# Two stage boundaries of a fused transformer kernel: processed by halves of the tokens instead of all tokens at once

## The chip, the cores and the metric

The kernel runs on one core of a Trainium2 chip. Its time is the device time in microseconds (us) of one execution; the median of 3 runs was 1045.91 us. The engines of a core work side by side, each through its own list of instructions in order, and wait for one another through counters (semaphores): TensorE (PE in the profile; PEld is its loading of stationary operands), VectorE (DVE), ScalarE (ACT), GpSimd (POOL), and SyncE (SP), which issues most of the DMA transfers here.

## The reference, cut to what matters

A sequence of 256 tokens of width 1024 goes through two blocks, each of two layers. All is float32.

```python
def first_block(x, ...):
    for l in range(2):
        x = hybrid_layer(x, ...)           # ends in: x = x + square(relu(h2 @ w_up)) @ w_down
    return rmsnorm(x, g_final)

def second_block(x, pre_norm_g, post_norm_g, ...):
    for i in range(2):
        h = rms_norm(x, pre_norm_g[i])
        y = even_mixer(h, ...) if i == 0 else odd_mixer(h, ...)
        x = x + rms_norm(y, post_norm_g[i])
    return x

def even_mixer(h, w_in, ...):
    z = h @ w_in                           # 1024 x 3072: six groups of 512 columns
    ...                                    # attention, pooling, gates
    return concatenate([att, pool]) @ w_out

def odd_mixer(h, w_in, ...):
    z = h @ w_in                           # 1024 x 2560: su, gc, ca, cb, gd of 512 columns each
    ...                                    # su goes into a state space scan, ca/cb into a convolution
    return concatenate([ssm_out, conv_out]) @ w_out
```

The "first boundary" is what lies between the last product of the first block (w_down of layer 1) and the even mixer's first product: the residual sum, rmsnorm with g_final, rms_norm with pre_norm_g[0]. The "second boundary" lies between the even mixer's w_out and the odd mixer's first product (su): rms_norm with post_norm_g[0], the residual sum, rms_norm with pre_norm_g[1].

## The kernel before, in words

The 256 tokens are two tiles of 128 tokens (`T = 2`); x and h lie in the core's memory with tokens on the partitions. Every product is made of pieces: a piece is a 512 x 512 block of a weight matrix, loaded by one DMA of 1 MB into one of four raw places. Since a fast float32r product alone is not exact enough, ScalarE copies a piece to a rounded upper part `w_hi` (line 1154), VectorE makes the remainder `w_lo = raw - w_hi` (line 1494; for the few pieces in `POOL_PIECES` GpSimd does it, line 2156), and TensorE adds three products: hi*hi, hi*lo and lo*hi. There are three places for split pieces (`SPLIT_RING = 3`), so ScalarE may split piece p only when TensorE has used up piece p - 3. In the ScalarE and VectorE programs `step(p)` splits piece p + 2. That order is written out by hand and strictly kept: an engine that waits at one instruction holds up all that stand behind it.

The activations need the same: `turn_rows` transposes h on TensorE (line 813; 16 transposes of 128 x 128 into four banks, each bank holding both token tiles), `turn_hi` on ScalarE (line 1182) copies the banks to `hT_hi` and `turn_lo` on VectorE (line 1515) writes the remainder `hT_lo`, both multiplying by the norm's factor g, which after the transposition is one number for each partition (`gain=V_PRE`).

Products come in two forms. In `tokens_out` the stationary operand is a 128 x 128 block of hT (one token tile) and 512 columns of the weights move past it, 128x512 a time. In `features_out` the stationary operand is a 128 x 128 block of the weights and the 256 tokens move past it, 128x256 a time; its result has features on the partitions. For a piece `tokens_out` makes 12 matmuls for each token tile (4 blocks by 3 products), and `features_out` 48 (4 by 4 by 3).

At the first boundary (pieces of the last `mlp_down`, then E_PIECE and E_PIECE + 1): for each half c of the columns VectorE adds tile 0, then tile 1 to x (line 1750) and multiplies by g_final (1756); ScalarE sums the squares of both (1172, 1349); `final_means` turns these into two means (lines 1665 to 1669), GpSimd takes the roots (line 2007), `final_rows` scales h (1675). TensorE meanwhile makes 12 products of a constant (`keep_clock`, line 780), and then waits for h. Behind the boundary ScalarE splits E_PIECE + 2, takes an exponential for the state space part (line 1357), and VectorE writes x = xg * rstd (line 1767).

At the second boundary (pieces E_OUT_PIECE to E_OUT_PIECE + 3, then O_PIECE and O_PIECE + 1): the result of w_out comes in two halves c of the columns, two pieces each. `post_squares` on ScalarE (line 1408) and `post_norm` on VectorE (1870, 1879) handle half 0 of both tiles, split three pieces, and handle half 1 of tile 0 and of tile 1. Then `squares` (1172), the root (2007), and the scaling of h (1890). TensorE transposes the matrices of the state space part (1039, 1044), runs 11 `keep_clock` products, and transposes h. The first product is su, by `features_out`, with `drive(0)` (1063) in it: 16 small products that start the state space part. VectorE answers each `drive(j)` with `turn_back(j)` (1908 to 1914) and `scan(j)` (1923); before `turn_back(0)` stand the splits of O_PIECE + 2 and O_PIECE + 3.

Of the kernel before, what the change touches and what calls it, by code (L numbers as in the profile page):

```python
# [94 lines left out]
POOL_PIECES = (O_PIECE + 4, O_PIECE + 5, O_PIECE + 8, O_OUT_PIECE, O_OUT_PIECE + 1)  # L95
# [8 lines left out]
V_MIX, V_MLP, V_PRE, V_LRE, V_LIM, V_PSC, V_D, V_GLUB, V_LNG, V_LNB, V_ROWS = (  # L104
    0, 16, 32, 48, 64, 80, 84, 88, 96, 100, 104)
# [50 lines left out]
def build_program(nc, ins, consts, where, out):  # L156
    ctx = ExitStack()
    with ctx:
# [55 lines left out]
        final_inv = sb("final_inv", [P, T])  # L214
        ret_ss = sb("ret_ss", [P, T, RET_HEADS])
# [99 lines left out]
        g_post = [area(10240, D), area(0, D)]  # L315
        conv_out = area(8192, HALF, SEQ)
# [21 lines left out]
        ROWS_T = [bank[:, i, :] for i in (6, 7, 3, 4)]  # L338
        ACC = [[bank[:, 2, :], bank[:, 3, :]], [bank[:, 4, :], bank[:, 5, :]]]
# [9 lines left out]
        poolw_landed = sem("poolw_landed")  # L349
        gpost_landed = [sem(f"gpost_landed{i}") for i in range(DEPTH)]  # L350
# [164 lines left out]
        def stat_count(n, t):  # L515

            return T * (n if n <= 2 * DEPTH else n - 1) + t + 1

# [68 lines left out]
        def _(sp):  # L587
# [4 lines left out]
            def small_inputs():  # L592
# [5 lines left out]
                vector_rows(V_PRE, ins["pre_norm_g_2"].rearrange("l d -> (l d)"))  # L598
# [27 lines left out]
            for l in range(DEPTH):  # L626
# [9 lines left out]
                for f in range(-2, F_GROUPS):  # L636
                    if l == DEPTH - 1 and f == 0:
                        for t in range(T):
                            sp.wait_ge(out_free[t], l * USES + USE_UP)
                        sp.dma_start(g_final, ins["g_final"].partition_broadcast(P)).then_inc(gfinal_landed, 16)  # L640
                        for b, w in enumerate(("o_b_re_2", "o_b_im_2")):
                            sp.dma_start(b_in[:, b, :, :], ins[w][0].rearrange("(s g) p i -> (g p) s i", g=2)).then_inc(s5_landed, 16)
# [19 lines left out]
            sp.dma_start(g_post[0], ins["post_norm_g_2"][0].partition_broadcast(P)).then_inc(gpost_landed[0], 16)  # L662
            for g in range(5):
# [28 lines left out]
        def _(pe):  # L692
# [131 lines left out]
            def turn_vectors():  # L824

                pe.wait_ge(rows_landed, 16 * 9)
# [111 lines left out]

            def mlp_down(l, f):
# [15 lines left out]
            for l in range(DEPTH):  # L955
# [25 lines left out]
                for f in range(F_GROUPS):  # L981
                    mlp_down(l, f)
# [4 lines left out]
            keep_clock(6, 12)  # L987
            turn_rows(h, lambda t: h_ready, lambda t, i: 2 * t + i // 2 + 1, groups=(range(4),))
            for g in range(3):
                tokens_out(E_USE + g, E_PIECE + 2 * g, 2, hT_hi, hT_lo, turn=4 * DEPTH if g == 0 else None)  # L990
# [42 lines left out]
            for c in range(2):  # L1033
# [450 lines left out]
        def _(dve):  # L1484
# [193 lines left out]
            for l in range(DEPTH):  # L1678
# [62 lines left out]
                for c in range(2):  # L1741
                    if c == 0 or l < DEPTH - 1:
                        step(p + DOWN_PIECE[F_GROUPS - 1] + c)
                    for t in range(T):
# [7 lines left out]
                        if l == DEPTH - 1:  # L1752
# [4 lines left out]
                            if c == 1:  # L1757
                                if t == T - 1:
                                    final_rows(0, 0)
# [443 lines left out]
```

## Time and profile before

| | |
|---|---|
| median of 3 runs | 1045.91 us (1045.83 to 1046.03) |
| the profiled execution | 1045.75 us, its span 1044.0 us |
| TensorE busy | 1026.6 us, 98% of the span |
| VectorE, ScalarE, GpSimd busy | 67%, 49%, 18% |
| TensorE's granted clock | 0.998 of full speed |

Times within the profile are counted from the start of the span. A row of the timeline gives the start, the duration, the engine, the line of the kernel, the operation, output and inputs, the shapes, how many instructions are merged in it, and, in brackets, how long the engine had been idle and what ended that. A matmul's record is longer than its share of the engine: they are pipelined, so what one costs is read as the distance between starts.

### The profile page before, as it was taken

The page shows a single profiled execution, that of the slowest core. Times are in us where ns is not written, and L with a number is a line of the kernel's source. Part 1 is how long each engine was busy: PE and PEld are TensorE (multiplying, and loading weights), DVE is VectorE, ACT ScalarE, POOL GpSimd, SP SyncE. Part 2 cuts the span into 40 slices and gives each one's busy share as a digit, 9 for nine tenths or more (in the row PEclk, how much of TensorE's full clock was granted, in tenths as well). Part 3 has the DMA queues.
Part 4 walks back from the last instruction along what each step waited for, and adds up shares of the span by engine and source line. Part 5 has one row for each costly group of instructions (what it writes and reads, how often), then busy time and mean ns, then how long its engine had stood idle before and what let it go on. Part 6 is the DMA issues. An engine that isn't in the chain of part 4 may idle for free. (4 is left out here: it accounts for less than half of the span.)

```text
span 1044.0 us, 14946 instructions
## 1 busy us (share of the span) xinstructions
PE 1026.6 (98%) x6343; PEld 892.8 (86%) x6343; DVE 704.2 (67%) x789; ACT 508.0 (49%) x630; POOL 187.4 (18%) x134
## 2 busy tenths in 40 slices
PE   9999999999999999999999999999999999999997
PEld 7888888899999998887888899999997899898686
DVE  4777646765555546777646666788848566789875
ACT  5545554464444445545554464444566453643352
POOL 0530010000000000530010020000000059278731
PEclk9999999999999999999999999999999999999999
DMA  9663444555555554663444566654563635236442
GB/s 345 227 214 127 160 161 161 166 185 177 200 182 181 188 193 133 203 212 126 157 162 161 168 190 209 199 190 174 163 227 120 223 125 175 92 117 177 116 142 81
DMA packets 97331, 180.33 MB, mean 173 GB/s; under 512 B 8584, under 2 KB 13552, under 8 KB 97136
## 3 DMA queue, kind: packets, MB, share of 16 engines
q1 hardware_dynamic: 97088, 179.28, 51.9%
q8 instruction: 50, 0.82, 0.3%
q10 hardware_dynamic: 176, 0.09, 0.0%
q14 instruction: 17, 0.14, 0.0%
HBM read 175.98 MB, written 1.05 MB: 170 GB/s over the span
## 5 line engine op out<-in xcount | busy, mean ns | idle before, releaser
L1494 DVE TENSOR_TENSOR w_lo<-raw,w_hi 128x2048 fp32r<-128x2048 f32 (+1 forms) x83 | 195.0, 2350 | 128.9 <-ACT w_hi L1154 126.5
L1494 DVE TENSOR_TENSOR w_lo<-arena,w_hi 128x2048 fp32r<-128x2048 f32 (+1 forms) x76 | 175.0, 2307 | 117.3 <-ACT w_hi L1154 117.2
L1154 ACT ACTIVATE w_hi<-raw 128x2048 fp32r<-128x2048 f32 (+1 forms) x88 | 166.6, 1893 | 147.1 <-PE bank L711 124.1
L708 PE MATMUL bank<-hT_hi,w_hi 128*128 128x256 f32 x816 | 232.0, 285 | 1.2 <-DVE arena L1975 0.7
L710 PE MATMUL bank<-hT_lo,w_hi 128*128 128x256 f32 x792 | 224.1, 283 | 0.0
L711 PE MATMUL bank<-hT_hi,w_lo 128*128 128x256 f32 x792 | 224.1, 283 | 0.0
L708 PE MATMUL bank<-w_hi,hT_hi 128*128 128x512 f32 (+1 forms) x552 | 214.4, 388 | 1.0 <-DVE w_lo L1494 0.7
L1154 ACT ACTIVATE w_hi<-arena 128x2048 fp32r<-128x2048 f32 (+1 forms) x76 | 143.6, 1890 | 118.3 <-PE bank L711 118.3
L711 PE MATMUL bank<-w_hi,hT_lo 128*128 128x512 f32 (+1 forms) x500 | 191.3, 383 | 0.0
L710 PE MATMUL bank<-w_lo,hT_hi 128*128 128x512 f32 (+1 forms) x500 | 191.3, 383 | 0.0
L708 PEld LDWEIGHTS bank<-hT_hi,w_hi 128*128 128x128 f32 x816 | 156.4, 192 | 4.7 <-issue 3.0
L710 PEld LDWEIGHTS bank<-hT_lo,w_hi 128*128 128x128 f32 x792 | 151.9, 192 | 0.5
L711 PEld LDWEIGHTS bank<-hT_hi,w_lo 128*128 128x128 f32 x792 | 151.9, 192 | 0.0
L708 PE MATMUL bank<-w_hi,uT_hi 128*128 128x512 f32 x352 | 137.5, 391 | 1.5 <-DVE uT_lo L1831 0.6
L710 PE MATMUL bank<-w_lo,uT_hi 128*128 128x512 f32 x352 | 137.1, 390 | 0.0
L711 PE MATMUL bank<-w_hi,uT_lo 128*128 128x512 f32 x352 | 137.0, 389 | 0.0
L708 PEld LDWEIGHTS bank<-w_hi,hT_hi 128*128 128x128 f32 x552 | 103.8, 188 | 23.2 <-issue 1.9
L711 PEld LDWEIGHTS bank<-w_hi,hT_lo 128*128 128x128 f32 x500 | 94.0, 188 | 18.5
L710 PEld LDWEIGHTS bank<-w_lo,hT_hi 128*128 128x128 f32 x500 | 94.0, 188 | 17.9
L2007 POOL TENSOR_TENSOR rstd<-mean,const 128x1 f32<-128x1 f32 (+1 forms) x16 | 9.9, 622 | 544.6 <-DVE mean L1503 372.9
L708 PEld LDWEIGHTS bank<-w_hi,uT_hi 128*128 128x128 f32 x352 | 66.1, 188 | 16.0 <-issue 2.9
L711 PEld LDWEIGHTS bank<-w_hi,uT_lo 128*128 128x128 f32 x352 | 66.1, 188 | 14.0
(296 smaller groups left out, 1136.9 us busy)
## 6 DMA issues: line engine op xcount, KB each, us to landing
arena<-in_w_in SPq DMA_DIRECT2D x22, 1024.0 KB, 5.2
raw<-in_w_in SPq DMA_DIRECT2D x21, 1024.0 KB, 5.0
arena<-in_w_up SPq DMA_DIRECT2D x16, 1024.0 KB, 5.3
raw<-in_w_up SPq DMA_DIRECT2D x16, 1024.0 KB, 5.2
arena<-in_w_down SPq DMA_DIRECT2D x16, 1024.0 KB, 5.1
raw<-in_w_down SPq DMA_DIRECT2D x16, 1024.0 KB, 5.0
raw<-in_o_w_in SPq DMA_DIRECT2D x8, 1024.0 KB, 5.9
raw<-in_e_w_in SPq DMA_DIRECT2D x6, 1024.0 KB, 5.1
```

What stands on the lines that cost most here:

```text
L708: pe.matmul(dst, a_hi, b_hi, start=first, stop=False, skip_group_check=shared)
L710: pe.matmul(dst, a_hi, b_lo, start=False, stop=False, skip_group_check=shared)
L711: mm = pe.matmul(dst, a_lo, b_hi, start=False, stop=last_one, skip_group_check=shared)
L1154: act.activation(w_hi[:, p % SPLIT_RING, :, 0:n], raw_at(p)[:, :, 0:n], copy).then_inc(hi_ready, 1)
L1494: dve.tensor_tensor(w_lo[:, s, :, 0:n], raw_at(p)[:, :, 0:n], w_hi[:, s, :, 0:n].bitcast(F32), ALU.subtract).then_inc(lo_ready, 1)
L2007: pool.tensor_tensor(dst, src, tab("minus_half")[:, 0:n], ALU.pow).then_inc(done, 1)
```

## The change

- The last `mlp_down` goes by token tile: tile 0 with both pieces, then tile 1 with both (`mlp_last`). Tile 0's h is transposed ahead of the last 3 matmuls of tile 1. `even_first` makes the even mixer's first group for tile 0 with both pieces, transposes tile 1, and does the same for tile 1. No `keep_clock` stands there any longer.
- The norm's factors g are no longer applied after the transposition but to the rows of h: two more transfers of 512 KB spread the vectors over the partitions (`g_pre`), and `final_rows` and `pre_rows` multiply by them with three-operand instructions on VectorE. `tile_hi` and `tile_lo` are then plain copies and remainders of 128x512.
- The remainder of E_PIECE + 1 goes from VectorE to GpSimd, between the root of tile 0 and that of tile 1. The scaling x = xg * rstd goes from VectorE to ScalarE, behind `tile_hi(0, 1)` and ahead of the exponential.
- The second half of w_out goes by token tile. `odd_first` makes su for the 128 tokens of tile 0, then for those of tile 1; only the products of `w_lo` with `hT_hi` of the second piece are made once for all 256 tokens.
- The remainder of O_PIECE + 1 is made in two halves on VectorE, ahead of `pre_rows(1)`; the orders of the small operations follow the tiles.

The diff, cut to what these points and the prediction speak of (the last two stretches of it are the lists of ScalarE and of GpSimd):

```diff
+            def mlp_last(l):
+                f = F_GROUPS - 1
+                pe.wait_ge(up_lo, 2 * (l * F_GROUPS + f + 1))
+                for t in range(T):
+                    at = slice(t * P, (t + 1) * P)
+                    for c in range(2):
...
+                        if t == T - 1 and c == 1:
+                            products(parts[:3], False, False)
+                            turn_tile(0, 0)
+                            products(parts[3:], False, True).then_inc(piece_used, 1)
+                        else:
+                            products(parts, False, True).then_inc(down0_done if t == 0 else piece_used, 1)
+            def odd_first(middle):
...
+                for t in range(T):
+                    at = slice(t * P, (t + 1) * P)
+                    if t:
+                        turn_tile(1, t)
+                    for b, js in enumerate(((0, 1), (2, 3))):
...
+                        part(w_hi, hT_hi, 0, js, at, first=(t == 0))
+                        part(w_lo, hT_hi, 0, js, at)
+                        if t and b:
+                            middle()
+                        pe.wait_ge(turned_lo, tile_turns(1, t, 0))
+                        last = part(w_hi, hT_lo, 0, js, at)
+                        if t and b:
+                            last.then_inc(piece_used, 1)
...
+                        part(w_hi, hT_hi, 1, js, at)
+                        pe.wait_ge(turned_lo, tile_turns(1, t, 1))
+                        part(w_hi, hT_lo, 1, js, at)
+                        if t:
+                            piece_ready(p + 1)
+                            part(w_lo, hT_hi, 1, js, slice(0, SEQ)).then_inc((out0_done, piece_used)[b], 1)
...
-            keep_clock(6, 12)
-            turn_rows(h, lambda t: h_ready, lambda t, i: 2 * t + i // 2 + 1, groups=(range(4),))
-            for g in range(3):
+            even_first()
+            for g in range(1, 3):
...
-            for c in range(2):
-                tokens_out(E_OUT_USE + c, E_OUT_PIECE + 2 * c, 2, uT_hi, uT_lo, halves=(1, 0), rows_ready=(2, 4))
+            tokens_out(E_OUT_USE, E_OUT_PIECE, 2, uT_hi, uT_lo, halves=(1, 0), rows_ready=(2, 4))
+            for t in range(T):
+                out_ready(E_OUT_USE + 1, t)
+                for i in range(2):
+                    p = E_OUT_PIECE + 2 + i
+                    piece_ready(p)
...
-            keep_clock(3, 11)
-            pe.wait_ge(s5_mats, 3)
-            turn_rows(h, lambda t: h_ready, lambda t, i: 2 * T + 2 * t + i // 2 + 1, groups=(range(4),))
+            turn_tile(1, 0)
...
-            features_out(O_USE + SU, O_PIECE + 2 * SU, 2, hT_hi, hT_lo, turn=4 * DEPTH + 1, after={(1, 2): lambda: drive(0)})
+            odd_first(lambda: drive(0))
...
+            step(E_OUT_PIECE)
+            for t in range(T):
+                even_squares(t, 0)
+            step(E_OUT_PIECE + 1)
+            step(E_OUT_PIECE + 2)
+            even_squares(0, 1)
+            pre_squares(0)
+            split(O_PIECE + 1)
+            even_squares(1, 1)
+            tile_hi(1, 0)
+            pre_squares(1)
...
+            inverse_roots(2 * DEPTH, 0, 2)
+            split(E_PIECE + 1)
+            inverse_roots(2 * DEPTH, 1, 2)
```

ScalarE at the first boundary, before: the split of E_PIECE + 1, the squares of x (`h_sb,ssq`) and of x * g_final (`arena,ssq`), the copies of the transposed h, the split of E_PIECE + 2, the exponential, the split of E_PIECE + 3, and the first result of the even mixer taken out of its bank.

```order
L1154 ACTIVATE w_hi<-raw 128x2048 [waits piece_used,raw_landed1]
L1172 ACTIVATE h_sb,ssq<-x_sb 128x512 [waits x_mlp]
L1349 ACTIVATE arena,ssq<-arena 128x512 [waits xg_ready]
...
L1182 ACTIVATE hT_hi<-bank,vec 128x256 [waits turned]
...
L1154 ACTIVATE w_hi<-arena 128x2048 [waits piece_used,raw_landed2]
L1357 ACT_TABLE_LOAD
L1357 ACTIVATE s_small<-s_small 128x16 [waits s5_decay_in]
L1154 ACTIVATE w_hi<-arena 128x2048 [waits piece_used,raw_landed3]
L1166 ACTIVATE arena<-bank 128x512 [waits out0_done,final_scaled]
```

And now:

```order
L1275 ACTIVATE w_hi<-raw 128x2048 [waits piece_used,raw_landed1]
L1293 ACTIVATE h_sb,ssq<-x_sb 128x512 [waits x_mlp]
L1483 ACTIVATE arena,ssq<-arena 128x512 [waits xg_ready]
L1311 ACTIVATE hT_hi<-bank 128x4x128 [waits turned] x2
L1293 ACTIVATE h_sb,ssq<-x_sb 128x512 [waits x_mlp]
L1483 ACTIVATE arena,ssq<-arena 128x512 [waits xg_ready]
L1275 ACTIVATE w_hi<-arena 128x2048 [waits piece_used,raw_landed2]
L1311 ACTIVATE hT_hi<-bank 128x4x128 [waits turned] x2
L1496 ACTIVATE x_sb<-arena,rstd 128x1024 x2
L1498 ACT_TABLE_LOAD
L1498 ACTIVATE s5_small<-s5_small 128x16 [waits s5_decay_in]
L1275 ACTIVATE w_hi<-arena 128x2048 [waits piece_used,raw_landed3]
```

The copies of tile 0 now stand between the squares of tile 1, and the split of E_PIECE + 2 stands ahead of tile 1's copies; the scaling of x stands between them and the exponential.

TensorE at the second boundary and in su, before: the transposes of the state space matrices, `keep_clock`, the transposes of h, and the start of su.

```order
L1039 MATMUL bank<-const,arena 128x128 x8
L1044 MATMUL bank<-const,arena 128x128 x8
L780 MATMUL bank<-const 128x128 x11
L813 MATMUL bank<-const,h_sb 128x128 x16
```

And now, from the start of su for tile 0 to its start for tile 1 and a part of that:

```order
L956 MATMUL bank<-const,h_sb 128x128 x8
L1016 MATMUL bank<-hT_hi,w_hi 128x128 x8
L1016 MATMUL bank<-hT_hi,w_lo 128x128 x8
L1016 MATMUL bank<-hT_lo,w_hi 128x128 x8
...
L956 MATMUL bank<-const,h_sb 128x128 x8
L1016 MATMUL bank<-hT_hi,w_hi 128x128 x8
L1016 MATMUL bank<-hT_hi,w_lo 128x128 x8
L1016 MATMUL bank<-hT_lo,w_hi 128x128 x8
L1016 MATMUL bank<-hT_hi,w_hi 128x128 x8
L1016 MATMUL bank<-hT_lo,w_hi 128x128 x8
L1016 MATMUL bank<-hT_hi,w_lo 128x256 x8
```

Where su was 96 matmuls of 128x256, it is now 160 of 128x128 and 16 of 128x256.

## Rows read from the trace of the kernel before

**Rows 1.** Page, part 1: busy time, share of the span, instructions of each engine.
```profile
PE 1026.6 (98%) x6343; PEld 892.8 (86%) x6343; DVE 704.2 (67%) x789; ACT 508.0 (49%) x630; POOL 187.4 (18%) x134
```

**Rows 2.** Windows: length, then busy us (instructions) of each engine, granted clock, DMA.
```profile
791.10:798.45 7.35, 5.53 (x43) 4.54 (x41) 5.54 (x15) 3.11 (x10) 1.67 (x2) 1.00 0.52 177
898.70:906.40 7.70, 6.41 (x55) 5.90 (x54) 4.82 (x12) 6.54 (x18) 2.12 (x3) 1.00 0.19 70
919.70:995.00 75.30, 72.41 (x820) 60.72 (x819) 69.74 (x69) 26.95 (x25) 61.39 (x20) 1.00 0.47 130
```

**Rows 3.** Timeline of TensorE at the first boundary.
```profile
780.25 0.39 PE L711 MATMUL bank<-w_hi,uT_lo 128*128 128x512 f32 x1
...
791.13 0.39 PE L711 MATMUL bank<-w_hi,uT_lo 128*128 128x512 f32 x1
...
798.45 0.47 PE L708 MATMUL bank<-w_hi,hT_hi 128*128 128x512 f32 x1 [0.35 <-ACT hT_hi L1182]
...
810.00 0.39 PE L708 MATMUL bank<-w_hi,hT_hi 128*128 128x512 f32 x1
```

**Rows 4.** Timeline of the other engines at the first boundary.
```profile
792.27 0.21 DVE L1669 TENSOR_SCALAR mean<-mean,final_inv 128x1 f32<-128x1 f32 x1
...
792.62 0.73 POOL L2007 TENSOR_TENSOR rstd<-mean,const 128x2 f32<-128x2 f32 x1 [169.65 <-DVE mean L1669]
...
793.17 0.69 DVE L1756 TENSOR_TENSOR arena<-x_sb,arena 128x512 f32<-128x512 f32 x1
...
793.90 0.63 ACT L1349 ACTIVATE arena<-arena 128x512 f32<-128x512 f32 x1
...
794.66 0.16 DVE L1665 TENSOR_TENSOR mean<-ssq 128x1 f32<-128x1 f32 x1 [0.33 <-ACT arena L1349]
...
802.31 1.28 ACT L1357 ACT_TABLE_LOAD   x1
...
804.82 1.92 ACT L1154 ACTIVATE w_hi<-arena 128x2048 fp32r<-128x2048 f32 x1 [1.00 <-PE bank L711]
```

**Rows 5.** Timeline around the second half of w_out: ScalarE and VectorE.
```profile
888.08 0.60 ACT L1408 ACTIVATE arena<-bank 128x512 f32<-128x512 f32 x1 [2.03 <-PE bank L711]
...
888.67 1.91 ACT L1154 ACTIVATE w_hi<-arena 128x2048 fp32r<-128x2048 f32 x1
...
890.61 2.29 DVE L1494 TENSOR_TENSOR w_lo<-arena,w_hi 128x2048 fp32r<-128x2048 f32 x1 [1.11 <-ACT w_hi L1154]
...
896.24 0.60 ACT L1408 ACTIVATE arena<-bank 128x512 f32<-128x512 f32 x1 [0.74 <-PE bank L711]
...
902.33 0.88 DVE L1890 TENSOR_SCALAR h_sb<-x_sb,rstd 128x512 f32<-128x512 f32 x2
```

**Rows 6.** Timeline of TensorE at the second boundary and in su.
```profile
898.53 0.39 PE L711 MATMUL bank<-w_hi,uT_lo 128*128 128x512 f32 x1
...
899.63 1.04 PE L1044 MATMUL bank<-const,arena 128*128 128x128 f32 x8
...
906.41 0.35 PE L708 MATMUL bank<-hT_hi,w_hi 128*128 128x256 f32 x1 [0.36 <-ACT hT_hi L1182]
...
908.35 0.28 PE L708 MATMUL bank<-hT_hi,w_hi 128*128 128x256 f32 x1
...
912.55 0.28 PE L711 MATMUL bank<-hT_hi,w_lo 128*128 128x256 f32 x1
...
917.08 1.15 PE L1063 MATMUL bank<-arena,b_mat 32*128 32x256 f32 x16
```

**Rows 7.** Timeline behind su: split of O_PIECE + 3, start of `turn_back(0)`.
```profile
916.24 1.90 ACT L1154 ACTIVATE w_hi<-arena 128x2048 fp32r<-128x2048 f32 x1
...
920.59 1.22 DVE L1908 TENSOR_TENSOR arena<-bank,arena 128x1024 f32<-128x1024 f32 x1
```

**Rows 8.** Timeline of TensorE: plain float32 products, two records each.
```profile
791.36 2.84 PE L780 MATMUL bank<-const 128*128 128x128 f32 x24
```

**Rows 9.** Groups by line and form: remainders on GpSimd.
```profile
L2156 POOL TENSOR_TENSOR w_lo<-raw,w_hi 128x2048 fp32r<-128x2048 f32 x5 | 24.4, 4889 | 20.0 <-ACT w_hi L1154 10.9 <-DVE hT_lo L1983 9.1
```

More of the change, by code:

```diff
@@ L93 @@
 NORMS = 2 * DEPTH + 5
-POOL_PIECES = (O_PIECE + 4, O_PIECE + 5, O_PIECE + 8, O_OUT_PIECE, O_OUT_PIECE + 1)
+POOL_PIECES = (E_PIECE + 1, O_PIECE + 4, O_PIECE + 5, O_PIECE + 8, O_OUT_PIECE, O_OUT_PIECE + 1)
 RAW_RING = 4
@@ L349, in build_program @@
         poolw_landed = sem("poolw_landed")
+        gpre_landed = [sem(f"gpre_landed{i}") for i in range(DEPTH)]
         gpost_landed = [sem(f"gpost_landed{i}") for i in range(DEPTH)]
@@ L1761, in _ @@
-            final_rows(0, 1)
-            for half in range(2):
-                final_rows(T - 1, half)
-            split(E_PIECE + 1)
-            turn_lo(4 * DEPTH, gain=V_PRE)
-            for t in range(T):
-                dve.tensor_scalar(x[:, t, :], xg[:, t, :], rstd[:, fin, t:t + 1], None, ALU.mult).then_inc(final_scaled, 1)
+                        for t in range(T):
+                            if t == 0:
+                                dve.wait_ge(down0_done, 2 * l + c + 1)
+                            else:
+                                dve.wait_ge(piece_used, p + DOWN_PIECE[F_GROUPS - 1] + c + 1)
+                            add_mlp(l, t, c).then_inc(x_mlp, 1)
@@ new lines, in _ @@
+            final_means(0)
+            dve.wait_ge(piece_used, p + DOWN_PIECE[F_GROUPS - 1] + 1)
+            add_mlp(l, 1, 0).then_inc(x_mlp, 1)
+            final_rows(0)
+            final_gain(1, 0)
+            dve.wait_ge(piece_used, p + DOWN_PIECE[F_GROUPS - 1] + 2)
+            add_mlp(l, 1, 1).then_inc(x_mlp, 1)
+            final_gain(1, 1)
+            tile_lo(0, 0, 0)
+            final_means(1)
+            tile_lo(0, 0, 1)
+            final_rows(1)
+            p = E_PIECE
+            step(p)
@@ L1768, in _ @@
+            for i in range(2):
+                tile_lo(0, 1, i)
             dve.memset(pool_in[:, :, 0:POOL_PAD], 0.0).then_inc(pool_zero, 1)
@@ L1882, in _, with post_gain @@
-            post_norm(2 * DEPTH + 2, 0, E_OUT_USE, E_OUT_PIECE, post_ready, late=(O_PIECE + 1,),
-                      between=lambda: row_mean(2 * DEPTH + 3, 0))
-            for t in range(T):
-                if t:
-                    row_mean(2 * DEPTH + 3, t)
+            def post_gain(n, i, t, c):
+                at = slice(c * COLS, (c + 1) * COLS)
+                dve.wait_ge(sq_done[t], 2 * n + c + 1)
+                if c == 1:
+                    row_mean(n, t)
+                dve.tensor_tensor(h[:, t, at], OUT[t], g_post[i][:, at], ALU.mult).then_inc(out_free[t], 1)
@@ new lines, in post_add, with pre_rows @@
+            def post_add(n, use, t, ready):
+                dve.wait_ge(rstd_ready, stat_count(n, t))
+                dve.wait_ge(out_free[t], use + 2)
+                for half in range(2):
+                    to = slice(half * COLS, (half + 1) * COLS)
+                    dve.scalar_tensor_tensor(out=x[:, t, to], in0=h[:, t, to], scalar=rstd[:, n, t:t + 1],
+                                             in1=x[:, t, to], op0=ALU.mult, op1=ALU.add).then_inc(ready, 1)
+            def pre_rows(t):
```

307 lines of the change are left out of this document (207 added, 100 removed).

## The prediction

> **What bounds the kernel now.** I read the page first: TensorE is busy for 98% of the span [rows 1], so a stretch is worth only what TensorE loses in it. The windows by stage and TensorE's own timeline come next. At the first boundary the last matmul of the MLP starts at 791.13 us and the first with the new hT at 798.45; at a distance of (791.13 - 780.25) / 48 = 0.227 us for a 128x512 matmul [rows 3] the engine is free at 791.36 and so 7.1 us pass. Real work in them is 16 transposes, (1.04 - 0.27) / 7 = 0.11 us each by the eight of [rows 6] (the records are 0.27 long), 1.8 us; the rest is `keep_clock` and waiting, though the window counts 5.5 of 7.35 us as busy [rows 2]. The first group then starts its 48 matmuls at 798.45 and the next starts at 810.00: 11.55 for 10.9 us of work, 0.65 more lost. So 5.9 us are to be had here at most. At the second boundary 898.76 to 906.41 is 7.65 us, 32 transposes are 3.5 of it, and 4.1 us are to be had [rows 6]. Behind su, 919.70 to 995.00, VectorE is busy for 69.7 of 75.3 us and TensorE for 72.4 [rows 2]: there both run tight, and what starts their chain (`turn_back(0)`, 920.59 [rows 7]) decides when the stage ends.
>
> **First boundary, tile by tile.** I follow the chain with before's durations. Up to the last `mlp_down` nothing changes. Tile 0 now has both halves at 785.9 (24 matmuls after 780.5), so VectorE ends x * g_final of it at 787.9. From the start of its counterpart to the means is 794.66 - 793.17 = 1.5 us, from the last small operation to the root's end 793.35 - 792.27 = 1.1 [rows 4]; with the 0.5 us of small operations between, the root is there at about 790.3. The scaling with g is two three-operand passes of 0.7 us (as the 0.69 of the 128x512 product [rows 4]) behind a small product of 0.25: h halves at 791.3 and 792.0. Before, this pass took 0.44 a half [rows 5]; the factor g costs 0.5 us a tile. TensorE has arrived at the transposes at 790.7, waits 0.6 and 0.25 us, makes its last 3 matmuls, and is through at 793.1.
>
> ScalarE is next late: before it can copy tile 0 it must square tile 1's first half, whose xg VectorE makes only after `final_rows(0)`, at 792.7. It squares until 793.4 and copies 128x512 by 794.0. There the even mixer's first matmul starts, 4.5 us earlier than 798.45. The remainder of E_PIECE + 1 on GpSimd takes 4.9 us [rows 9] from 790.8: ready at 795.7, while TensorE needs it 12 matmuls after 794.0, at 796.7. It is hidden by 1 us; if both engines slow one another it costs up to that. Tile 1's root follows it (796.7 to 797.6), its h at 799.3, and TensorE, through with tile 0 at 799.5, finds it. Transposes 0.9, the wait for the copy 0.3, 24 matmuls: the first group ends at 806.1, where it was 810.0.
>
> Then a new wait. Tile 0's result leaves its bank only when ScalarE has gone through tile 1's copies (801.0), two scalings of 128x1024 (1.0 each, between the 0.63 for 512 [rows 4] and the 1.9 for 2048 [rows 5]), the table load and exponential (1.5), a split (1.9) and 0.6 for the bank itself: 807.0 (table and split in [rows 4]). So the second group starts at 807.0 and not at 806.1. Gain 3.0 us; I take 2.7, since GpSimd now works beside VectorE. Bounds: 1.2 (every hidden edge costs) and 5.9. TensorE has no loss worth naming from there to w_out, so it holds.
>
> **Second half of w_out.** Before, it ran piece by piece, so the second piece was needed 24 matmuls after the start at 898.76 - 48 x 0.227 = 887.9. Now it is needed after 12, at 890.6. But ScalarE squares tile 1's first half until 888.7, splits until 890.6, and VectorE's remainder is 890.61 to 892.9 [rows 5]; both lists are unchanged up to here. TensorE waits 2.3 us, tile 0 is complete at 895.7 (before: 896.0) and tile 1 at 901.1 (before: 898.76). Nearly all that tile 0 was to win is gone.
>
> From there ScalarE's square starts at 895.9, before at 896.24 [rows 5], where 902.33 was the start of the scaling of h; now without the matrices' copies in between it starts at 900.8 and gives h at 901.5 and 902.2. The transposes end at 902.9, ScalarE's copy lets su begin at 903.1: 3.3 us before 906.41.
>
> **su.** It was 96 matmuls at (912.55 - 908.35) / 35 = 0.12 us, 11.5 us. It becomes 160 of 128x128 and 16 of 128x256. No row shows a float32r matmul of 128 columns. A 128x512 costs 0.227 and a 128x256 0.12, so by columns alone 128 would cost 0.12 - 0.053 = 0.067 us: the lower bound. The upper is plain float32, two records of (2.84 - 0.28) / 23 = 0.111 for each product [rows 8], 0.223. The nearest row are the transposes, which have one stationary load for 128 moving columns as these have: 0.11. I take 0.11. The sum is then 160 x 0.11 + 16 x 0.12 = 19.5 us, 8.0 more.
>
> A page of the Trainium skill speaks to that price from both sides. "TensorE: Matmul & The Clock Gate", section "LDWEIGHTS (loading the stationary operand)", has a load take P / 1.2 ns whatever the rows, 107 ns for 128 columns; by that, halving the moving columns saves nothing, and the transposes' 0.11 agrees. The same page, "Back-to-back issue gap", gives about 81 ns for 128 columns in a stream of loads and matmuls; by that the 160 would be 13.0 us and not 17.6, the second rival.
>
> In time, with 0.11: tile 0 takes 80 matmuls to 911.9, the transposes of the matrices and of tile 1 go to 913.7 (h of tile 1 is there at 910), the copy to 914.05. Tile 1's first half is 32 x 0.11 + 0.96 = 4.5 us, then 16 matmuls, `drive(0)` (1.1 [rows 6]), 8 matmuls: O_PIECE is used up at 923.3. Only then may ScalarE split O_PIECE + 3 (1.9), and VectorE after it (2.3): `turn_back(0)` starts at 927.8 where it was 920.59 [rows 7], 7.2 us late. Before, that split started at 916.24 [rows 7]. su itself ends 6.3 us later, so the scan chain is the later of the two. What is moved besides (the second g vector's DMA, the halves of O_PIECE + 1's remainder, the orders behind the last product) has other work over it; I cost it at nothing, at most 1 us if that cover is gone.
>
> **Sum.** 1045.75 us for the profiled execution (its span 1044.0 and 1.75 around it) - 2.7 + 7.2 = 1050.3. The median of before is 1045.91, 0.16 above that execution, well inside what I can tell.
>
> **The rivals.**
> 1. Forecast, 56%: a 128-column matmul costs 0.10 to 0.13 us. 1050.3; with the bounds of the first boundary 1047 to 1054.
> 2. The short matmul is cheap, 24%: 0.067 to 0.085 us. With 0.067 tile 0 ends at 908.5, tile 1's h (910.0 to 910.5) becomes the wait, tile 1's copy is there at 910.7, O_PIECE is used up at 917.4 and `turn_back(0)` starts at 922.0, 1.4 late: 1045.75 - 2.7 + 1.4 = 1044.4; between 1041.5 and 1047 with the first boundary's bounds. For it speaks that 512 and 256 columns fit a line by columns; against it that the stationary load must fit under the moving columns, and the transposes do not show it. This is the side that ends faster; it decides once the price falls below 0.08. The page's 81 ns, put in, would give about 1045.3.
> 3. The short float32r product runs as plain float32, 14%: 0.223. Tile 0 ends at 920.9, O_PIECE is used up at 937.8, `turn_back(0)` at 942.4, 21.8 late: 1064.9. For it only that nobody sees such a form in the trace, and that a plain product of 128 columns is that dear.
> 4. The clock, 6%: `keep_clock` filled 2.8 us at the first boundary [rows 8]; now TensorE has waits of 0.6, 0.9 and 2.3 us with nothing in them. If the granted clock, 1.00 in all windows [rows 2], fell for some microseconds to the lower of its levels, matmuls there cost double: about 3 us on top, 1053.3. Against it: `keep_clock` gone, the waits are also shorter than the 7 us they replace.
>
> **How the numbers follow.** What a measurement can tell from no change is about 0.2%, 2.1 us: below 1043.8 and above 1048.0. Faster: 0.13 of case 2 and 0.02 from a first boundary at its best in case 1, 0.15. Same: 0.11 of case 2 and 0.06 of case 1, 0.17. Slower: 0.48 of case 1, cases 3 and 4, 0.68. The range 1042.5 to 1056 takes in cases 1, 2 and 4 and leaves out case 3 and some 4% of the rest; case 1's own is 1047 to 1054.
>
> **What would show it.** The profile after should have: the first 128x512 matmul with the new hT near 794, the second group near 807 and before it a wait for ScalarE; TensorE idle for 2.3 us inside the second half of w_out, waiting for `w_lo`; the first matmul of su near 903; a distance of 0.11 us between its 128x128 matmuls; `turn_back(0)` 7 us later against w_out's end than before, that is 927.8 - 2.7 in the span's time. The forecast fails if that distance is below 0.08 or above 0.14, or if the stage up to 995 takes up the late start instead of passing it on.

## The result and the profile after

The changed kernel took 1058.6 us (median of 4 executions, 1058.37 to 1063.07) against 1045.87 of the kernel before on the same chip: a ratio of 1.0131, 95% interval 1.0119 to 1.0143. It is slower by 12.7 us, where 4.4 were forecast. In a second series it took 1057.96 (ratio 1.0117, 1.0102 to 1.0132). The first profile is of the execution of 1063.07, which is 4.5 us above its neighbours, so the rows here are of the second series (span 1056.1 us); where the two part is told under run 1.

Timeline of TensorE, changed kernel, at the first boundary; it answers to [rows 3]:

```profile
790.71 0.39 PE L722 MATMUL bank<-w_hi,uT_lo 128*128 128x512 f32 x1
791.46 0.66 PE L956 MATMUL bank<-const,h_sb 128*128 128x128 f32 x4 [0.36 <-DVE h_sb L1849]
796.37 1.11 PE L956 MATMUL bank<-const,h_sb 128*128 128x128 f32 x4 [4.25 <-DVE h_sb L1849]
797.13 0.78 PE L719 MATMUL bank<-w_hi,uT_hi 128*128 128x512 f32 x1
797.71 0.63 PE L721 MATMUL bank<-w_lo,uT_hi 128*128 128x512 f32 x1
798.13 0.63 PE L722 MATMUL bank<-w_hi,uT_lo 128*128 128x512 f32 x1
798.56 0.63 PE L995 MATMUL bank<-w_hi,hT_hi 128*128 128x512 f32 x1
...
813.07 0.47 PE L719 MATMUL bank<-w_hi,hT_hi 128*128 128x512 f32 x1 [0.73 <-ACT arena L1287]
```

The first half of tile 0's h comes on time. The second lets TensorE wait for 4.25 us, and behind the wait a 128x512 matmul costs 0.43 us and not 0.227. The second group starts at 813.07, where 807.0 was forecast and the kernel before had 810.00 [rows 3].

Timelines of VectorE, GpSimd and ScalarE in the same place; they answer to [rows 4]:

```profile
790.65 5.66 DVE L1849 SCALAR_TENSOR_TENSOR h_sb<-arena,final_scale 128x512 f32<-128x512 f32 x2
796.23 0.68 DVE L1933 TENSOR_TENSOR arena<-x_sb,arena 128x512 f32<-128x512 f32 x1
```

```profile
791.15 4.61 POOL L2229 TENSOR_TENSOR w_lo<-raw,w_hi 128x2048 fp32r<-128x2048 f32 x1 [0.73 <-ACT w_hi L1275]
```

```profile
796.94 0.63 ACT L1483 ACTIVATE arena<-arena 128x512 f32<-128x512 f32 x1 [5.26 <-DVE arena L1933]
```

Two instructions that should take 1.4 us take 5.66, and they end 0.55 us behind GpSimd's remainder (791.15 to 795.76). VectorE is shown as busy, not as waiting: no view of waits names GpSimd here.

TensorE in the second half of w_out and in su; it answers to [rows 6]:

```profile
893.68 0.39 PE L722 MATMUL bank<-w_hi,uT_lo 128*128 128x512 f32 x1
896.26 0.50 PE L719 MATMUL bank<-w_hi,uT_hi 128*128 128x512 f32 x1 [2.19 <-DVE w_lo L1652]
...
905.96 0.39 PE L722 MATMUL bank<-w_hi,uT_lo 128*128 128x512 f32 x1
...
908.43 1.08 PE L1016 MATMUL bank<-hT_hi,w_hi 128*128 128x128 f32 x8 [0.34 <-ACT hT_hi L1311]
909.35 1.06 PE L1016 MATMUL bank<-hT_hi,w_lo 128*128 128x128 f32 x8
...
926.92 1.15 PE L1184 MATMUL bank<-arena,b_mat 32*128 32x256 f32 x16
...
931.73 0.28 PE L719 MATMUL bank<-hT_hi,w_hi 128*128 128x256 f32 x1
```

Windows of the stretches named (length, busy us and instructions of PE, PEld, DVE, ACT, POOL, granted clock, DMA share, GB/s); they answer to [rows 2]:

```profile
797.20:801.10 3.90, 3.90 (x11) 3.01 (x10) 2.08 (x4) 2.95 (x9) 0.00 (x0) 0.50 0.25 72
...
896.27:900.00 3.73, 3.73 (x10) 2.96 (x11) 2.14 (x1) 0.00 (x0) 0.00 (x0) 0.58 0.66 199
908.46:931.75 23.29, 23.04 (x209) 22.38 (x210) 10.97 (x15) 9.55 (x15) 4.44 (x3) 1.00 0.15 46
```

The wait for `w_lo` is the forecast one (2.19 us against 2.3). What was not in the sum is the clock: 0.50 behind the first wait, which is the level of 1.2 GHz, and 0.58 behind the second, mostly that level; 1.00 is 2.4 GHz. In su the records of eight start 0.89 to 0.92 us apart, 0.112 us for each 128x128 matmul, at full clock, and TensorE's loading of stationary operands (PEld) is busy for 22.38 of the 23.29 us.

Behind su; these answer to [rows 7], and the first gives all four `turn_back` (the count, durations in ns, first and last start):

```profile
L2108 DVE TENSOR_TENSOR arena<-bank,arena x4: 1200/1214/1225, 933.6 to 982.6; 128x1024 f32<-128x1024 f32 x4
```

```profile
929.20 1.92 ACT L1275 ACTIVATE w_hi<-arena 128x2048 fp32r<-128x2048 f32 x1 [3.32 <-PE bank L1016]
```

`turn_back(0)` starts at 933.6, 13.0 us later than before. The kernel ends 12.1 us later in span. So the loss lies ahead of `turn_back(0)`, and the rest passes it on.

### The profile page after: what moved, and what is told of

Read it like the earlier page. It is cut to its first block and busy times, and to the rows that moved or that the text cites. A ratio compares the mean times of both kernels' runs of the same rounds, so it can differ in the third digit from the quotient of the medians.

```text
span 1061.3 us, 15009 instructions
## 1 busy us (share of the span) xinstructions
PE 1034.7 (97%) x6377; PEld 899.2 (85%) x6377; DVE 706.2 (67%) x781; ACT 509.0 (48%) x624; POOL 189.0 (18%) x135
## 5 line engine op out<-in xcount | busy, mean ns | idle before, releaser
L1652 DVE TENSOR_TENSOR w_lo<-raw,w_hi 128x2048 fp32r<-128x2048 f32 (+1 forms) x81 | 191.3, 2362 | 127.1 <-ACT w_hi L1275 124.7
L719 PE MATMUL bank<-hT_hi,w_hi 128*128 128x256 f32 x784 | 223.0, 285 | 0.5 <-DVE arena L2175 0.5
L721 PE MATMUL bank<-hT_lo,w_hi 128*128 128x256 f32 x768 | 217.3, 283 | 0.0
L722 PE MATMUL bank<-hT_hi,w_lo 128*128 128x256 f32 x768 | 217.3, 283 | 0.0
L719 PE MATMUL bank<-w_hi,hT_hi 128*128 128x512 f32 (+1 forms) x536 | 208.2, 388 | 1.6 <-DVE w_lo L1652 0.9
L721 PE MATMUL bank<-w_lo,hT_hi 128*128 128x512 f32 (+1 forms) x492 | 188.1, 382 | 0.0
L719 PEld LDWEIGHTS bank<-hT_hi,w_hi 128*128 128x128 f32 x784 | 150.3, 192 | 3.3 <-issue 2.5
L721 PEld LDWEIGHTS bank<-hT_lo,w_hi 128*128 128x128 f32 x768 | 147.3, 192 | 0.5
L722 PEld LDWEIGHTS bank<-hT_hi,w_lo 128*128 128x128 f32 x768 | 147.3, 192 | 0.0
L719 PEld LDWEIGHTS bank<-w_hi,hT_hi 128*128 128x128 f32 x536 | 100.7, 188 | 23.3 <-issue 2.4
```

What stands on the lines that cost most here:

```text
L719: pe.matmul(dst, a_hi, b_hi, start=first, stop=False, skip_group_check=shared)
L721: pe.matmul(dst, a_hi, b_lo, start=False, stop=False, skip_group_check=shared)
L722: mm = pe.matmul(dst, a_lo, b_hi, start=False, stop=last_one, skip_group_check=shared)
L1652: dve.tensor_tensor(w_lo[:, s, :, 0:n], raw_at(p)[:, :, 0:n], w_hi[:, s, :, 0:n].bitcast(F32), ALU.subtract).then_inc(lo_ready, 1)
```

## Experiments

**1. The changed kernel again** (1057.96 us; the expectation's question was where the 4.5 us of the first profile lie).

> The changed kernel once more, as it is. Two readings are open of its profiled execution, which took 4.5 us longer than its other executions (1063.07 against 1058.4 to 1058.7). Theory: the instruction stream has places where a small shift decides a longer wait (the late stage, from 980 us on), and a second profile with a span near 1057 shows the losses at the first boundary (second three-operand instruction of line 1849 held, TensorE waits 4.2 us for it), in w_out (2.2 us) and in su unchanged, and 4 us less behind 980. Rival: the 4.5 us lie at the boundaries themselves, and the hold on line 1849 is short in this profile. Time 1058.5 by both.

The boundaries are equal in both profiles to 0.1 us, and `turn_back(0)` starts at 933.5 and 933.6. The theory holds and the rival falls. Row of the first profile, which answers to the one above:

```profile
L2108 DVE TENSOR_TENSOR arena<-bank,arena x4: 1200/1210/1225, 933.5 to 986.2; 128x1024 f32<-128x1024 f32 x4
```

The last `turn_back` starts 3.6 us later. ScalarE's splits show why; first the second profile, then the first:

```profile
978.06 1.91 ACT L1275 ACTIVATE w_hi<-raw 128x2048 fp32r<-128x2048 f32 x1 [4.11 <-DMA raw<-in_o_glu_w]
```

```profile
980.86 1.92 ACT L1275 ACTIVATE w_hi<-raw 128x2048 fp32r<-128x2048 f32 x1 [7.00 <-DMA raw<-in_o_glu_w]
```

The piece was asked for at the same time (969.58 and 969.47) and landed 2.8 us later in the first profile. It shares the queue with 16 transfers within the core's memory, and the DMA engines are full there (share 1.08 from 970 to 980) in both profiles, so the load alone doesn't explain the 2.8 us. In the first profile TensorE then waits 2.42 and 3.21 us for GpSimd (1.15 and 0.83 in the second), and behind the longer wait the clock falls a third time, as a window of it shows (granted clock 0.72):

```profile
1009.00:1015.00 6.00, 6.00 (x55) 4.43 (x46) 4.55 (x8) 0.42 (x1) 0.20 (x1) 0.72 0.52 145
```

**2. The remainder of E_PIECE + 1 on VectorE again**

```diff
             inverse_roots(2 * DEPTH, 0, 2)
-            split(E_PIECE + 1)          # GpSimd
...
             tile_lo(0, 0, 0)
+            split(E_PIECE + 1)          # VectorE
             final_means(1)
```

> The changed kernel, with the remainder of E_PIECE + 1 back on VectorE (behind the remainder of tile 0's first half of hT), nothing on GpSimd beside final_rows(0). Theory A (VectorE instruction with two inputs from the core's memory can't start while GpSimd's remainder runs): the pair of line 1849 takes 1.4 us instead of 5.7, TensorE's wait of 4.25 us falls to under 0.5, no half clock behind it; TensorE then waits about 1 us for the remainder and something for tile 1's h; the first group ends 3 to 5 us earlier, time 1054 to 1055.5. Rival (the pair is held by something else, as the transfer of the g vector or TensorE's use of the banks): the wait of about 4 us stays, and 2.3 us more on VectorE make it 1059 to 1060.5.

Measured 1053.60 us, ratio 1.0081 (1.0066 to 1.0096), 4.4 less than the changed kernel in the same series and 0.4 under theory A's range. TensorE, VectorE:

```profile
793.98 0.47 PE L995 MATMUL bank<-w_hi,hT_hi 128*128 128x512 f32 x1 [0.59 <-ACT hT_hi L1311]
797.76 0.50 PE L995 MATMUL bank<-w_hi,hT_hi 128*128 128x512 f32 x1 [0.78 <-DVE w_lo L1652]
...
808.38 0.47 PE L719 MATMUL bank<-w_hi,hT_hi 128*128 128x512 f32 x1 [0.73 <-ACT arena L1287]
```

```profile
790.58 1.41 DVE L1849 SCALAR_TENSOR_TENSOR h_sb<-arena,final_scale 128x512 f32<-128x512 f32 x2
```

The pair takes 1.41, the first even matmul starts at 793.98 (the prediction had 794.0), and the clock doesn't fall at this boundary (in w_out it still does, behind a wait of 2.19 us). Theory A holds; a cause in the transfer of g or in the banks would have stayed. TensorE still waits 0.78 us for the remainder, and 0.73 for ScalarE ahead of the second group. The second group is 4.7 us earlier than in the changed kernel and 1.6 earlier than before the change.

**3. The two waits filled**

```diff
+                    if ph == t == 0 and i == 1:
+                        keep_clock(7, 16)
                     pe.wait_ge(h_ready, 2 * T * ph + 2 * t + i + 1)
...
+                    if t == 0 and i == 1:
+                        keep_clock(6, 9)
                     piece_ready(p)
```

> The changed kernel, with 16 products of a constant between the two halves of tile 0's transposes (3.6 us, where TensorE waits 4.25) and 9 ahead of the wait for the fourth piece of w_out (2.0 us, where it waits 2.2). Theory B (TensorE's clock falls because it stands idle there, and costs 2.0 and 1.7 us): granted clock 1.00 in 796 to 801 and in 896 to 900, matmuls 0.227 us apart in both, su begins 3 to 4 us earlier, time 1054.5 to 1055.5. Rival (the clock falls for another reason, or the fall costs nothing since another chain is the later): time 1058 to 1059, with distances of 0.43 us still there or su beginning at the same time.

Windows of this kernel over both stretches:

```profile
796.30:801.10 4.80, 4.13 (x19) 3.22 (x20) 3.67 (x10) 4.13 (x9) 0.31 (x1) 1.00 0.46 126
894.80:898.50 3.70, 3.65 (x16) 3.01 (x17) 2.20 (x1) 0.57 (x2) 0.00 (x0) 1.00 0.68 207
```

The clock stays at 1.00 in both; the pair of line 1849 (here 1853) still takes 5.67. The second group starts at 811.64, 1.4 us earlier, and su at 905.42, 3.0 earlier: the two falls cost 1.4 and 1.6 us. The time, 1056.13 (ratio 1.0111, 1.0085 to 1.0137; one execution at 1061.5), is 1.8 under the changed kernel's and 0.6 above theory B's range, and the intervals overlap; that the clock costs 3 us up to su rests on the trace, not on the total. One execution of the changed kernel (1058.55 us, without a profile) has a mean granted clock of 0.997 where its neighbours have 0.994, and was no faster than they.

**4. su for all 256 tokens at once, the waits not filled**

```diff
-            odd_first(lambda: drive(0))
+            (transposes of c_pad)
+            turn_tile(1, 1)
+            features_out(O_USE + SU, O_PIECE + 2 * SU, 2, hT_hi, hT_lo, turn=0, after={(1, 2): lambda: drive(0)})
```

> The changed kernel, with su made for all 256 tokens at once as before (96 matmuls of 128x256), behind the transposes of both tiles; the rest as changed. TensorE then waits some 4 us for tile 1's h (there at about 915), but su is 11.5 us instead of 22.4. Theory D (the 160 short matmuls are the largest loss): su ends 928 to 929.5 instead of 931.65, turn_back(0) starts 2 to 3 us earlier, time 1055.5 to 1057, less if the clock falls in the wait. Rival (what is late at turn_back(0) comes from h of tile 1 and the splits, not from the matmuls' number): turn_back(0) within 1 us of where it is, time 1058 to 1060.

Measured 1064.99 us, ratio 1.0186 (1.0169 to 1.0203): both theories missed the time, by 5 us and more. `turn_back(0)` is 2.1 us earlier, as theory D had it, but the four spread over 55.8 us and not 49.0:

```profile
L2121 DVE TENSOR_TENSOR arena<-bank,arena x4: 1199/1210/1224, 931.4 to 987.2; 128x1024 f32<-128x1024 f32 x4
```

```profile
970.29 1.91 ACT L1288 ACTIVATE w_hi<-raw 128x2048 fp32r<-128x2048 f32 x1 [10.42 <-DMA raw<-in_o_w_in]
980.80 1.91 ACT L1288 ACTIVATE w_hi<-raw 128x2048 fp32r<-128x2048 f32 x1 [6.21 <-DMA raw<-in_o_glu_w]
```

Here the last piece of o_w_in, asked for at 961.40, lands after 8.9 us among the transfers that start at 961.86, and the next piece is late as well. In run 1 the same piece was asked for at 963.20, also 0.46 us ahead of those transfers, and landed after 5.9 us: why it took 3 us longer here stays open. The clock fell in this run too, while TensorE waited 3.76 us for tile 1's h. This run can't tell what su costs; run 10 is its better form.

**5. and 6. The first boundary alone by tiles**, all behind it as before: with the remainder on GpSimd (5), and on VectorE (6).

> The kernel before with the change at the first boundary alone, as it stands in the change (remainder of E_PIECE + 1 on GpSimd); w_out, the second boundary and su as before. In the changed kernel the second group of the even mixer starts at 813.0 where it was 810.0, 3.0 us late. Theory: the rest passes this on, 1048 to 1049. Rival (the late start is taken up before the end, or meets another wait as the changed kernel's does): 1046, or over 1050.

> The same, with the remainder of E_PIECE + 1 on VectorE as in the run before that had it there. Its second group started at 808.4, 1.6 us earlier than in the kernel before. Theory: the gain is kept to the end, 1043.5 to 1044.5, the first version faster than the kernel before. Rival (the gain is lost at w_out or in the late stage, where a transfer lands at its own time): 1045 to 1046.

Measured 1048.66 us (ratio 1.0027, 1.0017 to 1.0037; 9 executions) and 1044.58 us (0.9983, 0.9973 to 0.9993; 10 executions, all from 1043.95 to 1044.71). The first lies in its theory's range, the second 0.08 us above it. The first boundary by tiles gains 1.4 us once GpSimd is out of VectorE's way, and loses 2.7 with it in the way.

**7. The kernel before without its fills**

```diff
-            keep_clock(6, 12)
...
-            keep_clock(3, 11)
```

> The kernel before without both fills (12 products of a constant at the first boundary, 11 at the second). Theory B (a TensorE that stands idle for some 2 to 4 us comes back at the lower clock): granted clock about 0.5 for 4 us behind both boundaries, 1.5 to 2 us lost at each, 1048.5 to 1049.5. Rival (the clock's fall in the changed kernel has another cause): 1045.5 to 1046.

Windows of this kernel behind either wait (TensorE stood for 2.85 and 0.60 us, then for 2.28):

```profile
798.00:802.00 4.00, 4.00 (x14) 3.27 (x13) 4.00 (x7) 4.00 (x9) 0.00 (x0) 0.54 0.22 39
...
905.00:909.00 4.00, 3.92 (x21) 3.18 (x20) 2.08 (x6) 2.85 (x8) 0.55 (x1) 0.69 0.00 0
```

The clock falls at both places, in a kernel that has nothing of the change. `turn_back(0)` starts at 922.1, 1.5 us late, less than the 3 to 4 I had expected. The time is 1052.94, 3.4 us above theory B's range, but it spreads from 1048.15 (the profiled execution) to 1054.2, ratio 1.0057 (1.0037 to 1.0076); the four long ones have no profile, so what makes 3 to 6 us more in them stays open.

**8. The second half of w_out by pieces**

```diff
-            tokens_out(E_OUT_USE, E_OUT_PIECE, 2, ...)
-            (second half: for each token tile, both pieces)
+            for c in range(2):
+                tokens_out(E_OUT_USE + c, E_OUT_PIECE + 2 * c, 2, uT_hi, uT_lo, halves=(1, 0), rows_ready=(2, 4))
```

> The changed kernel with the second half of w_out piece by piece as before (both tiles for the third piece, then both for the fourth). Theory C: the wait of 2.2 us for the remainder of the fourth piece and the low clock behind it are gone, tile 1 is complete at 902.1 instead of 906.1; tile 0 is complete at 899.4 instead of 900.8, and since su waits for tile 0's h it starts 1.4 us earlier only: 1056 to 1057. Rival (TensorE's longer wait for tile 0's h lowers the clock in its place, in su): no gain, 1058.

Four executions: 1055.6, 1057.1, 1065.1 and 1070.5 us, median 1061.1; ratio 1.0153 (1.0092 to 1.0214). The wait for `w_lo` is gone and w_out ends at 902.0, as expected. The profiled execution is the longest, and its timeline of TensorE shows the rival in a form I had not priced:

```profile
905.02 1.32 PE L956 MATMUL bank<-const,h_sb 128*128 128x128 f32 x8 [2.02 <-DVE h_sb L2049]
...
907.48 1.91 PE L1016 MATMUL bank<-hT_hi,w_lo 128*128 128x128 f32 x8
```

A window of the same stretch:

```profile
909.00:925.00 16.00, 16.00 (x77) 16.00 (x77) 3.85 (x6) 1.77 (x6) 1.52 (x1) 0.50 0.20 67
```

After a wait of 2.02 us the clock fell, and su's 128-column matmuls then ran at 0.213 us each from 907.5 to 926, with TensorE busy all the while. The mean granted clock of the four executions goes the same way: 0.985 and 0.988 in the two long ones, 0.995 and 0.996 in the two short ones, which have no profile. So the same wait doesn't always cost this much.

**9. and 10. Step by step from the second boundary.** Run 9: the remainder on VectorE, w_out by pieces, 8 products of a constant ahead of tile 0's transposes. Run 10: that, and su at once, its waits filled with 7 and 16 more.

> The changed kernel with the remainder of E_PIECE + 1 on VectorE, the second half of w_out piece by piece, and 8 products of a constant ahead of tile 0's transposes at the second boundary. What is left of the change's loss should be su alone. Theory D (su's 128-column products are the largest part): su begins at 901.7 and ends at 925, turn_back(0) starts near 927, 1051 to 1052. Rival (w_out's order and the low clock are the larger part): su ends the same, but the time is under 1048.

> The same, with su for all 256 tokens at once behind the transposes of both tiles, and the waits ahead of them filled with 7 and 16 products of a constant, so that the clock stays. Theory D: tile 1's h is there at 906, su begins at 907 and ends near 920, turn_back(0) starts within 1 us of 920.6, time 1044.5 to 1046.5, 5 to 7 us under the run with su by tiles. Rival (the gain is lost in the late stage, as in the run that made su at once and left the waits unfilled: turn_back(0) 2 us earlier and yet 7 us longer): 1050 or more.

Measured 1053.19 us (ratio 1.0076, 1.0060 to 1.0092) and 1047.97 us (1.0020, 1.0011 to 1.0030; ten executions within 0.9 us). First run 9, then run 10:

```profile
L2097 DVE TENSOR_TENSOR arena<-bank,arena x4: 1198/1214/1224, 926.7 to 979.4; 128x1024 f32<-128x1024 f32 x4
```

```profile
L2112 DVE TENSOR_TENSOR arena<-bank,arena x4: 1198/1215/1224, 922.8 to 972.6; 128x1024 f32<-128x1024 f32 x4
```

su by tiles costs 3.9 us at `turn_back(0)` and 5.2 in the time. Both times are a little above their expectations (1.2 and 1.5 us): in run 9 the `turn_back`s spread over 52.7 us again (and a wait of 2.37 us ahead of 986.3 has the lower clock behind it), and in run 10 tile 1's h came at 907.7 instead of 906.

**11. The first boundary alone, tuned**: run 6 with the remainder in two halves, the first in the gap where VectorE waits for tile 1's last product, and x = xg * rstd on VectorE.

```diff
             final_gain(1, 0)
+            order.mark(first_half(0))
...
             tile_lo(0, 0, 0)
-            split(E_PIECE + 1)
+            first_half(1).then_inc(lo_ready, 1)
...
+            for t in range(T):      # VectorE, behind tile_lo(0, 1); gone from ScalarE
+                dve.tensor_scalar(x[:, t, :], xg[:, t, :], rstd[:, fin, t:t + 1], None, ALU.mult).then_inc(final_scaled, 1)
```

> The first boundary alone by tiles, the remainder of E_PIECE + 1 on VectorE in two halves (the first in the gap where VectorE waits for tile 1's last product), and the scaling of x back on VectorE, behind tile 1's remainder. In the version without these two edits TensorE waits 0.8 us for the remainder and 0.7 us for ScalarE ahead of the second group. Theory: both waits go, the second group starts at 807, 1043.0 to 1043.6 against 1044.58. Rival (the late stage lands on its own time): no change, 1044.5.

Measured 1043.28 us, ratio 0.9972 (0.9961 to 0.9983), as theory had it: the fastest here, and faster than both kernels. TensorE:

```profile
806.98 0.47 PE L717 MATMUL bank<-w_hi,hT_hi 128*128 128x512 f32 x1
```

The second group starts at 806.98 without a wait, 3.0 us ahead of 810.00 [rows 3].

**12. GpSimd's remainder in four instructions**

```diff
-            split(E_PIECE + 1)
+            for k in range(KP):
+                part = pool.tensor_tensor(w_lo[:, s, k, :], raw_at(E_PIECE + 1)[:, k, :], w_hi[:, s, k, :].bitcast(F32), ALU.subtract)
```

> The changed kernel, with GpSimd's remainder of E_PIECE + 1 as four instructions of 128x512 instead of one of 128x2048. Theory A (each engine's instruction keeps the other's out for its whole length): VectorE's second instruction of line 1849 is held for one quarter, 1.1 us, and not for 4.3: the pair takes 2.5 to 3 us, TensorE waits 1.2 to 1.6 us instead of 4.25, 1055.5 to 1056.5. Rival 1 (the port goes to GpSimd as long as it has work): the pair takes 5.7 as before, 1058. Rival 2 (they only slow one another): the pair takes about 2.5 and GpSimd's four take longer than 4.6 in sum.

Measured 1055.75 us, ratio 1.0096 (1.0080 to 1.0112), in theory A's range. VectorE and GpSimd:

```profile
790.61 2.43 DVE L1849 SCALAR_TENSOR_TENSOR h_sb<-arena,final_scale 128x512 f32<-128x512 f32 x2
792.96 1.77 DVE L1933 TENSOR_TENSOR arena<-x_sb,arena 128x512 f32<-128x512 f32 x1
794.65 0.74 DVE L1828 SCALAR_TENSOR_TENSOR x_sb<-bank,rstd,x_sb 128x512 f32<-128x512 f32 x1
```

```profile
791.11 6.45 POOL L2362 TENSOR_TENSOR w_lo<-raw,w_hi 128x512 fp32r<-128x512 f32 x4 [0.73 <-ACT w_hi L1275]
```

The pair is held for 1.0 us and the next instruction for 1.1, each about one quarter (4.61 / 4 = 1.15), while the instruction whose first input lies in a matmul bank takes its usual 0.74. GpSimd's four span 6.45 instead of 4.61 and so wait in their turn. The engines take turns by whole instructions: theory A. Rival 1 falls; rival 2's sign, GpSimd's longer sum, is there, but the holds have the length of an instruction.

The trace of this run also bounds what runs 3 and 7 say of the clock. At the first boundary TensorE waited only 1.02 and 1.67 us, and the 128x512 matmuls behind that were 0.43 us apart. In w_out it waited 2.19 us for `w_lo`, just as in run 1, and the clock stayed at 1.00, with 0.23 us from one matmul to the next:

```profile
895.33 0.50 PE L719 MATMUL bank<-w_hi,uT_hi 128*128 128x512 f32 x1 [2.19 <-DVE w_lo L1652]
895.67 0.40 PE L721 MATMUL bank<-w_lo,uT_hi 128*128 128x512 f32 x1
895.90 0.40 PE L722 MATMUL bank<-w_hi,uT_lo 128*128 128x512 f32 x1
```

So the length of a wait of about 2 us doesn't settle whether the clock falls behind it. The mean clock of the four executions of this kernel lies between 0.995 and 1.000 too (1056.1 us and 1053.2 us).

## Why the prediction was wrong

The direction held; the size did not, and the time lies outside the range. The way to `turn_back(0)`, forecast for the span at 927.8 - 2.7 = 925.1 and measured at 933.6, step by step:

| step of the prediction | forecast | measured | late |
|---|---|---|---|
| second group of the even mixer starts (810.0 - 2.7) | 807.3 | 813.07 | 5.8 |
| from there, w_out ends (901.1 - 2.7) | 898.4 | 906.2 | 7.8, so 2.0 more |
| su begins (903.1 - 2.7) | 900.4 | 908.4 | 8.0 |
| `turn_back(0)` | 925.1 | 933.6 | 8.5 |

Of the 8.5 us, 3.3 are the hold on VectorE (4.7 in run 2 less the 1.4 of the clock), 3.0 the clock behind the two waits (run 3), 1.1 the rest of the first boundary (808.38 in run 2 against 807.3), and 1.1 are small parts behind it.

- **The step that failed** is "The remainder of E_PIECE + 1 on GpSimd takes 4.9 us ... It is hidden by 1 us; if both engines slow one another it costs up to that." The remainder was not in TensorE's way but in VectorE's: it kept out h's second half, and TensorE with it, for 4.3 us. Without it the second group comes 4.7 us earlier (run 2). In place of the 2.7 us that the sum took as gained here, the changed kernel lost 3.1 (813.07 against 810.00). I bounded the cost by TensorE's slack for `w_lo`, when the chain that decides ran through VectorE. The trace of before held the price, in a row of GpSimd and one of VectorE that the prediction left out:

```profile
946.19 2.20 POOL L2100 TENSOR_TENSOR arena<-arena 128x1024 f32<-128x1024 f32 x1 [1.96 <-ACT arena L1166]
946.56 3.97 DVE L1494 TENSOR_TENSOR w_lo<-raw,w_hi 128x2048 fp32r<-128x2048 f32 x1
```

  A remainder of 2.29 us took 3.97 beside a GpSimd instruction that ended at 948.39, and 948.39 + 2.29 is 950.7, near its end at 950.5. The Trainium skill states it too, in "SBUF — State Buffer", section "Who interferes with whom": a VectorE instruction with two inputs from the core's memory and a GpSimd instruction that reads it lock one another out for a whole instruction, and the first to start wins. Runs 2 and 12 agree with it.
- **The clock** was rival 4, at 6% and about 3 us. The price was right (1.4 and 1.6 us, run 3), the form was wrong: it isn't another way in which the case could go but a term on top of the forecast, and the sum had it at nothing. My argument against it, that the waits are shorter than the 7 us they replace, did not count that `keep_clock` had stood in those. In run 7 waits of 2.85 and 2.28 us had the lower clock behind them; in run 12 one of 2.19 had not, so the term is likely and not certain for each wait.
- **w_out** was right: a wait for `w_lo` of 2.19 us against 2.3, and with it the loss of nearly all that tile 0 was to win.
- **su's price** was right: 0.112 us for a 128-column matmul against 0.11 taken, so that rivals 2 and 3 fall. From su's start to `turn_back(0)` it was 24.7 forecast, 25.1 measured. Rival 1's condition was thus met, and its time still missed. One term is written wrong: "32 x 0.11 + 0.96 = 4.5" leaves out 8 matmuls. Tile 1's first half has 40 of 128x128, 5.4 us, and took 5.5; the 923.3 of the forecast agrees with 40, but the 937.8 of rival 3 comes from 32 and should be 1.8 later.
- **Rest of the first boundary**: with GpSimd out of the way it came at 793.98 (forecast 794.0) and 808.38 (807.0).
- **What passes on.** From the last `turn_back` to the end it is 75.0 to 75.1 us in the three profiles whose clock falls at 1009 to 1017 (the first of the changed kernel and those of runs 4 and 8), and 73.0 to 73.5 in all others, run 9 with its fall at 986.8 among them. From the first to the last it is 49.0 to 51.3 in ten profiles (50.3 in the kernel before), and 52.7 or 55.8 in the other four, by when the pieces land. So the late start passes on, as forecast, and now and then 3 us and more are added that I had not allowed for.

Where the 13.0 us at `turn_back(0)` lie, by taking parts back one after the other: 4.7 the remainder on GpSimd with the clock behind it (run 2: 928.9), 2.2 w_out by tiles with its clock (run 9: 926.7), 3.9 su by tiles (run 10: 922.8), 2.9 the rest of the second boundary by tiles (run 6: 919.9); less 0.7 that the first boundary gains. The rest of the second boundary was not taken apart, and why a piece among the 16 transfers lands 3 to 4 us later in some executions wasn't settled.

## What to carry to other kernels

Before a piece of work is moved to GpSimd, look at what VectorE does beside it and whether those instructions read two inputs from the core's memory; the price is up to the length of GpSimd's instruction, put on VectorE's chain. Count the clock as a term of its own behind each bare wait of TensorE: here waits of 4.25 and 2.19 us cost 1.4 and 1.6 us more, though not every wait of about 2 us did. Check what a fill was for before it goes. Splitting a product by token tiles paid where the tokens are the stationary side and the next piece was ready (the 128x512 products of the first boundary: 2.5 us gained in run 11). It lost in the second half of w_out, where the tokens are stationary too but the next piece is needed after 12 matmuls instead of 24 and its remainder came 2.19 us late. It lost in su, where the tokens move: half the columns cost 0.112 us where all of them cost 0.12, so the 160 + 16 matmuls add up to 19.8 us where the 96 took 11.5.

## What the runs showed of the hardware

- A VectorE instruction with two inputs from the core's memory was held until GpSimd's ended (5.66 us for two of 0.7 beside one of 4.61; 2.43 beside quarters of 1.15). Beside the quarters, two instructions with an input in a matmul bank kept their 0.74 and 0.68.
- A float32r matmul with 128 stationary rows and 128 moving columns, a new stationary operand each time, takes 0.112 us at 2.4 GHz and 0.213 at 1.2. The Trainium skill's 81 ns ("TensorE: Matmul & The Clock Gate", section "Back-to-back issue gap") was not reached in any run. The same page, "LDWEIGHTS (loading the stationary operand)", has a load take P / 1.2 ns, an estimate of 107 ns for 128 columns; the 0.112 us at 2.4 GHz are near it, the 0.213 at 1.2 GHz are twice that.
- Over the 14 profiles, TensorE's waits of 3.2 to 4.3 us had the granted clock of 0.50 behind them in all nine cases, those of 2.0 to 2.9 us in eight of thirteen. TensorE was mostly back at 1.00 some 3 to 7 us after it went on (4.9 and 3.9 in run 1; 7.2 and 3.3 in run 7, the 3.3 with 128x128 transposes); in su's stream of 128x128 matmuls it stayed at 0.50 for 16 us and more in the profile of run 8. What decides between these was not found.
